# A decoder-trunk step: the last expert pass written out with its own code and an on-chip product, and the state-space input matrices laid out by the host

## The reference

```python
mod = dot(silu(c), ada_w) + ada_b            # 9 condition vectors -> shift, scale, gate, twice
h = LN(x) * (1 + scale1) + shift1
q, k, v, u = split(dot(h, w_in))             # attention beside a state-space layer on u
bbr = cr[..., None] * br - ci[..., None] * bi  # input matrices b_re, b_im: 64 groups x 64 states x 16 channels
x = LN(ALPHA * x + gate1 * o) * ln1_g + ln1_b
h2 = LN(x) * (1 + scale2) + shift2
# hierarchical mixture of 32 experts: each row goes to 2 of them, with weights comb
act = silu(h2 @ w_gate[e]) * (h2 @ w_up[e]) * comb[:, e]
f = sum_e act @ w_down[e]                    # w_gate, w_up: 2048 x 512, w_down: 512 x 2048, each 4 MB
y = LN(ALPHA * x + gate2 * f) * ln2_g + ln2_b
```

## Time and profile before

| | us |
|---|---|
| median of 3 runs | 1608.94 (1608.58 to 1610.85) |
| the profiled execution's own time | 1608.62 |
| its span | 1606.8 |
| TensorE busy in the span | 1493.3 (93%) |
| VectorE, ScalarE, GpSimd busy | 509.9, 288.0, 142.6 |
| DMA | 559.66 MB, 348 GB/s on average |

### The profile page before, as it was taken

How to read it: one execution, slowest core, us unless ns; L and a number is a source line. 1 busy time by engine, 2 the same in 40 slices (tenths; PEclk the granted TensorE clock), 3 DMA queues, 4 the chain that set the end, 5 groups by cost and what they waited for, 6 DMA issues and landing times.

```text
span 1606.8 us, 22161 instructions
## 1 busy us (share of the span) xinstructions
PE 1493.3 (93%) x8151; PEld 645.8 (40%) x8152; DVE 509.9 (32%) x1446; ACT 288.0 (18%) x669; POOL 142.6 (9%) x213
## 2 busy tenths in 40 slices
PE   3999999999999999999999999999999999999974
PEld 2557544455444445333333433333433333333321
DVE  6648344322343347821211212121121211112116
ACT  2221240143123222111211101010010100001011
POOL 6001000321300230000000000000000000000011
PEclk9999999999999898899999999999999999999987
DMA  9995888972487699899999899999979999999955
GB/s 297 381 387 191 308 324 311 317 195 94 168 300 291 220 361 399 363 409 422 421 422 421 333 385 422 422 421 422 422 291 420 421 421 422 422 421 422 422 229 214
DMA packets 119286, 559.66 MB, mean 348 GB/s; under 512 B 15657, under 2 KB 20553, under 8 KB 64921
## 3 DMA queue, kind: packets, MB, share of 16 engines
q1 hardware_dynamic: 100800, 510.20, 79.7%
q0 software_dynamic: 17952, 46.05, 8.5%
q10 hardware_dynamic: 482, 2.70, 0.6%
HBM read 565.78 MB, written 42.37 MB: 378 GB/s over the span
## 4 chain that ended last, share of the span: by engine, by line
PE 79%; DMA 13%; DVE 3%; ACT 2%; issue 1%; POOL 0%; SPq 0%; POOLq 0%; DVEq 0%; ACTq 0%
PE bank L793 24%; PE bank L810 11%; DMA ring<-in_exp_w_up 8%; PE bank L2431 6%; PE bank L755 6%; PE bank L2315 5%; PE bank L2165 4%; PE bank L348 3%; DMA ring<-in_ada_w 3%; PE bank L2358 2%; PE bank L762 2%; DMA ring<-in_w_in 2%; DVE BC L611 1%; PE bank L801 1%; PE bank L2143 1%
## 5 line engine op out<-in xcount | busy, mean ns | idle before, releaser
L793 PE MATMUL bank<-ring,BC 128*64 128x512 f32 x1984 | 470.6, 596 | 5.5 <-DMA ring<-in_exp_w_up 3.2
L793 PEld LDWEIGHTS bank<-ring,BC 128*64 128x64 f32 x1984 | 153.3, 137 | 296.5 <-issue 273.9
L810 PE MATMUL bank<-ring,BC 128*64 128x512 f32 x992 | 219.7, 595 | 16.7 <-ACT BC L716 16.7
L590 DVE COPY MOD<-bank 128x512 f32<-128x512 f32 x32 | 22.1, 692 | 429.0 <-PE bank L762 429.0
L755 PE MATMUL bank<-H,MOD 128*64 128x512 f32 x512 | 131.1, 592 | 0.3 <-DVE H L2025 0.3
L810 PEld LDWEIGHTS bank<-ring,BC 128*64 128x64 f32 x992 | 70.8, 137 | 142.5 <-issue 142.5
L546 POOL DMA_INDIRECT y_dram<-BC,y_row x31 | 30.0, 968 | 946.1 <-DVE y_row L620 861.1
L2431 PE MATMUL bank<-ring,MT 128*128 128x512 f32 x224 | 101.4, 601 | 0.3 <-ACT BC L1381 0.3
L704 ACT COPY MOD<-bank 128x512 f32<-128x512 f32 x32 | 18.8, 587 | 460.3 <-PE bank L762 460.3
L2315 PE MATMUL bank<-ring,MT 128*128 128x512 f32 x192 | 85.4, 598 | 1.0 <-ACT X L1230 1.0
L617 DVE COPY BC<-bank 128x512 f32<-128x512 f32 x31 | 21.5, 692 | 166.1 <-PE bank L810 166.1
(11 more groups left out here) (561 smaller groups left out, 1462.7 us busy)
## 6 DMA issues: line engine op xcount, KB each, us to landing
ring<-in_exp_w_gate SPq DMA_DIRECT2D x128, 1024.0 KB
ring<-in_exp_w_up SPq DMA_DIRECT2D x128, 1024.0 KB
ring<-in_exp_w_down SPq DMA_DIRECT2D x128, 1024.0 KB
ring<-in_ada_w SPq DMA_DIRECT2D x96, 1024.0 KB
ring<-in_w_in SPq DMA_DIRECT2D x20, 1024.0 KB
y_dram<-con POOLq DMA_DIRECT2D x20, 1024.0 KB, 34.2
ring<-in_w_out SPq DMA_DIRECT2D x16, 1024.0 KB
ring<-in_ssm_glu_w SPq DMA_DIRECT2D x4, 1024.0 KB
```

What stands on the lines that cost most here:

```text
L793: mm = pe.matmul(bank[64 * i:64 * i + 64, 2, :], xT[:, q // 2, k % 4, 64 * (q % 2):64 * (q % 2) + 64], ring[:, at, 512 * (k % 4):512 * (k ...
L810: mm = pe.matmul(bank[64 * (c % 2):64 * (c % 2) + 64, 4 + c // 2, :], aT[:, j, :], ring[:, at, 512 * c:512 * c + 512], start=(j == 0), sto ...
```

## The change

1. **Last pass.** The loops run one pass less, and each engine has straight code for the last one. On TensorE this code leaves out the gathering and the transposes of a next pass, and puts in their places the products that spread gate2 (before in the tail), and three transposes of a selection matrix. The result of the last pass is not written to DRAM: it is copied to `YS`, and a matmul with the transposed selection `SWT` (weight where a row's slot is in this pass, else 0) puts it into the output banks, before the gathered results are added to them. The weights in `DW` are 0 for rows that the last pass has (`live`).
2. **Gathers.** ScalarE signals `y_all` when the writes of the passes before the last have landed and the last pass's ninth chunk (the first of down) is used. The gathers go to slots 6 to 9 and 10 of the ring, not 0 to 5.
3. **Start.** The host lays b_re and b_im out as one tensor of 128 rows of 4 KB, loaded by one DMA. The table is cleared by four memsets on VectorE, first in its program, and not on GpSimd. VectorE copies the transposed conditions (`ct_ready`) after the first decay steps.

```diff
@@ expert_loops
-            with eng.Fori(start, start + FULL) as it:
+            with eng.Fori(start, start + FULL - 1) as it:
...
-            with eng.Fori(start + FULL, start + NBLK) as it:
-                with eng.If(extra > it - (start + FULL)):
+            with eng.Fori(start + FULL - 1, start + NBLK - 1) as it:
+                with eng.If(extra > it - (start + FULL - 1)):
@@ moe_dve
-            for b in range(3):
-                for i in range(2):
-                    V.tensor_scalar(DW[:, b, i, :], ident, cwt[:, b, i:i + 1], None, ALU.mult).then_inc(S("dw_ready"), 1)
...
-            expert_loops(dve, body)
+            last = expert_loops(dve, body) + FULL - 1
+            at, live = rsm[:, 0, :, 0:2], rsm[:, 1, :, 0:2]
+            go(V.tensor_scalar(at, slot_f[:, :, :], 2.0 * SLOTS, None, ALU.add),
+               V.scalar_tensor_tensor(out=live, in0=slot_f[:, :, :], scalar=-2.0 * SLOTS, in1=cwt[:, :, :],
+                                      op0=ALU.is_lt, op1=ALU.mult))
+            iota = spread_mid(con[:, C_IOTA:C_IOTA + SLOTS], 2)
+            for b in range(3):
+                w = [t.rearrange("p (h s) -> p h s", h=2) for t in (SW[:, b, :], SW2)]
+                go(*[V.tensor_scalar(w[i], iota, at[:, b, i:i + 1], cwt[:, b, i:i + 1], ALU.is_equal, ALU.mult)
+                     for i in range(2)])
+                V.tensor_tensor(w[0], w[0], w[1], ALU.add).then_inc(S("dw_ready"), 1)
+                dve.wait_ge(S("dw_ready"), b + 1)
+            for b in range(3):
+                for i in range(2):
+                    V.tensor_scalar(DW[:, b, i, :], ident, live[:, b, i:i + 1], None, ALU.mult).then_inc(S("dw_ready"), 1)
+            dve.wait_ge(S("sg_ready"), last + 1)
+            V.tensor_tensor(AC[hi, :], SG[hi, :], bank[hi, 2, :], ALU.mult).then_inc(S("act_ready"), 1)
+            dve.wait_ge(S("y_written"), 16 * last + Y_FILLED)
+            dve.wait_ge(used, last * RING + len(plan) + RING)
+            V.tensor_copy(YS[:, 1, :], bank[:, 5, :]).then_inc(S("dw_ready"), 1)
@@ moe_act
-            act.wait_ge(S("y_written"), 16 * (extra + FULL) + Y_FILLED)
+            last = expert_loops(act, body) + FULL - 1
+            for i in range(5):
+                act.wait_ge(S("g2_ps"), i + 1)
+                dst = G2[:, 512 * i:512 * i + 512] if i < 4 else G2s
+                nc.scalar.copy(dst, bank[:, G2_BANKS[i], :]).then_inc(S("g2_ready"), 1)
+            act.wait_ge(S("g2_ps"), 6)
+            nc.scalar.copy(SWT.rearrange("p b t -> p (b t)"), bank[:, 0, 0:3 * P]).then_inc(S("g2_ready"), 1)
+            act.wait_ge(used, last * RING + len(plan) + 8)
+            nc.scalar.activation(SG[hi, :], bank[0:64, 2, :], ACT.Silu).then_inc(S("sg_ready"), 1)
+            act.wait_ge(S("at_ps"), last + 1)
+            nc.scalar.copy(aT, bank[:, 3, 0:256].rearrange("p (j s) -> p j s", j=4)).then_inc(S("at_ready"), 1)
+            act.wait_ge(S("y_written"), 16 * last + Y_FILLED)
+            act.nop()
+            act.wait_ge(used, last * RING + len(plan) + 9)
             act.nop().then_inc(S("y_all"), 1)
+            act.wait_ge(used, last * RING + len(plan) + RING)
+            nc.scalar.copy(YS[:, 0, :], bank[:, 4, :]).then_inc(S("g2_ready"), 1)
@@ moe_pe: last_weights(k) is called between the products of the last pass, as next_rows(e, k) in the others
+                if k == 4:
+                    pe.wait_ge(S("mod_ready"), 5)
+                    gate2(0)
+                    gate2(1)
+                elif k == 8:
+                    gate2(2)
+                    gate2(3)
+                elif k == 12:
+                    pe.wait_ge(S("g2_ready"), 2)
...
+                    pe.wait_ge(S("dw_ready"), 3)
+                    for b in range(3):
+                        mm = pe.transpose(bank[:, 0, P * b:P * b + P], SW[:, b, :], ident)
+                    mm.then_inc(S("g2_ps"), 1)
...
-            expert_loops(pe, body)
+            last = expert_loops(pe, body) + FULL - 1
+            place = place_of(last)
+            gate_up(last, place, last_weights)
+            down(last, place)
             tail_pe(pe)
 
-        Y = ring[:, 0:6, :].rearrange("p (b i) d -> p b i d", i=2)
+        Y = ring[:, 6:10, :].rearrange("p (b i) d -> p b i d", i=2)
@@ tail_pe
+            pe.wait_ge(S("g2_ready"), 7)
+            pe.wait_ge(S("dw_ready"), 10)
+            def last_rows(b, q, at):
+                h = slice(64 * (q % 2), 64 * (q % 2) + 64)
+                t = slice(32 * q, 32 * q + 32) if b == 2 else slice(0, P)
+                pe.matmul(bank[t, at, :], SWT[h, b, t], YS[h, q // 2, :], start=True, stop=False)
+            for q in range(4):
+                last_rows(2, q, 7)
+            for b in range(2):
+                for q in range(4 - b):
+                    last_rows(b, q, Y_BANKS[b][q])
@@ the start: gpsimd, then vector
-                for i, s in ((0, "ssm_b_re"), (1, "ssm_b_im")):
-                    for h in range(2):
-                        pool.dma_start(Braw[64 * h:64 * h + 64, i, :, :],
-                                       a[s][0].rearrange("(q h) n c -> h n q c", h=2)[h]).then_inc(S("b_in"), 16)
+                pool.dma_start(Braw.rearrange("p c q n -> p (c q n)"), a["ssm_b_rows"]).then_inc(S("b_in"), 16)
...
-                nc.gpsimd.memset(later[:, 0:8192], 0.0).then_inc(S("ab_clear"), 1)
...
-                dve_chain.settle(dve)
-                dve.wait_ge(S("ct_ps"), 1)
-                V.tensor_copy(cT[:, :, 0:NROW], bank[:, 7, 0:KD * NROW].rearrange("p (k r) -> p k r", k=KD))\
-                 .then_inc(S("ct_ready"), 1)
+                for i in range(3):
+                    dve_chain.tick(V.memset(ring[:, PRE_RING + i, :], 0.0))
+                V.memset(ring[:, PRE_RING + 3, :], 0.0).then_inc(S("ab_clear"), 1)
+                dve.wait_ge(S("con_in"), 16)
```

More of the change, by code:

```diff
@@ L772, in turn, with next_rows, gate2, last_weights @@
                 mm.then_inc(S("turn_ps"), 1)
-            def body(e):
-                place = pe.value_load(rint[0:1, bass.ds(e + I_PLACE, 1)], min_val=0, max_val=E - 1)
+            def next_rows(e, k):
+                if k == 4:
+                    pe.wait_ge(S("sel_ready"), e + 2)
+                    gather_rows(0, 0)
+                    gather_rows(0, 1)
+                elif k == 8:
+                    gather_rows(1, 0)
+                    gather_rows(1, 1)
+                elif k == 12:
+                    gather_samples()
+            def gate2(x):
+                r = slice(32 * x, 32 * x + 32)
+                pe.matmul(bank[:, G2_BANKS[x], :], con[r, C_SEL:C_SEL + P], MOD[r, 3, :], start=True, stop=True)\
+                  .then_inc(S("g2_ps"), 1)
+            def last_weights(k):
+                if k == 4:
+                    pe.wait_ge(S("mod_ready"), 5)
+                    gate2(0)
+                    gate2(1)
+                elif k == 8:
+                    gate2(2)
+                    gate2(3)
+                elif k == 12:
+                    pe.wait_ge(S("g2_ready"), 2)
+                    for g in range(4):
+                        r = slice(32 * g, 32 * g + 32)
+                        mm = pe.matmul(bank[r, G2_BANKS[4], :], con[r, C_SEL + P:C_SEL + P + NS], MOD[r, 3, :],
+                                       start=True, stop=True)
+                    mm.then_inc(S("g2_ps"), 1)
+                    pe.wait_ge(S("dw_ready"), 3)
+                    for b in range(3):
+                        mm = pe.transpose(bank[:, 0, P * b:P * b + P], SW[:, b, :], ident)
+                    mm.then_inc(S("g2_ps"), 1)
+            def gate_up(e, place, between):
                 pe.wait_ge(S("xg_ready"), 2 * e + 2)
                 for k in range(KD):
[L778 to L786, removed]
+                    between(k)
                     for i in range(2):
@@ L796, in body, with down @@
                             mm.then_inc(used, 1)
-                turn(e + 1)
+            def down(e, place):
                 pe.wait_ge(S("rint_ready"), since("rint_ready") + 4)
@@ L812, in body, with place_of @@
                     mm.then_inc(used, 1)
+            def place_of(e):
+                return pe.value_load(rint[0:1, bass.ds(e + I_PLACE, 1)], min_val=0, max_val=E - 1)
+            def body(e):
+                place = place_of(e)
+                gate_up(e, place, lambda k: next_rows(e, k))
+                turn(e + 1)
+                down(e, place)
             gather_first(0)
@@ L821, in moe_pe @@
             pe.wait_ge(S("rint_ready"), since("rint_ready") + 4)
[L822 removed]
+            last = expert_loops(pe, body) + FULL - 1
+            place = place_of(last)
+            gate_up(last, place, last_weights)
+            down(last, place)
             tail_pe(pe)
[L825 to L826 removed]
+        Y = ring[:, 6:10, :].rearrange("p (b i) d -> p b i d", i=2)
+        Yq, xq, mq = [ring[:, 10, 512 * i:512 * i + 512] for i in range(2)], X[:, 2, 0:512], st[:, 2, :]
```

(10 more changed lines are left out.)

24 lines of the change are left out of this document (8 added, 16 removed).

## The result

The changed kernel takes 1598.12 us (median of 4 runs, 1596.48 to 1598.97) against 1609.09 (4 runs, 1608.58 to 1610.85): a ratio of 0.9929, 95% interval 0.9916 to 0.9942. That is 11.0 us less; the forecast was 14.4 less.

A forecast was written before the change was run, and what follows sets the result against it. Chain bound 79% by the matrix engine, 13% by DMA; span 1606.8 - 4.5 (start) - 9.9 (tail) = 1592.4, + 1.8 around it + 0.3 to the median = 1594.5 us; range 1589 to 1602.

The forecast's parts named there:

- rival 2: Start: 64-byte runs cost only what the page's rule says, a gain of 1.8 us instead of 4.5; 1597.2 us, chance 0.12.
- (a): Start: b_re and b_im in 4 KB rows instead of 64-byte runs; later chunks land 4.5 us earlier, bounds 0 and 6.
- (b): Start: GpSimd's memset cost VectorE 2.4 to 7.5 us; moving it has the first block ready at 32.3, not 34.7.
- Rival 3: Start: VectorE's memsets (7 us) hold GpSimd up, so its first loads come late; about 1600 us, chance 0.08.
- (c): Ahead of the last pass: leaving the loop takes 4.0 us, the lower clock 2.3; the pass is 2.9 us later.
- Rival 1: Loop exit costs nothing: clock stays up or the pass catches up with weights; 2.9 us earlier, 1591.6 us, chance 0.2.
- Rival 5: Last pass: straight code fetched behind queued weights, TensorE starts it at 1550 instead of 1527; about 1617 us, chance 0.07.
- (d): Tail: gathers issued from 1551.8, not 1559.98; last product ends at 1578.5, not 1588.4, a gain of 9.9 us.

The follow-up runs named there:

- c_rows: Changed kernel with c_re and c_im also laid out by the host, one load in 8 KB rows, no clearing of Cw: 1597.46 us, ratio to before 0.9926.
- tail_alone: Changed kernel with four loads for b_re and b_im and the clearing on GpSimd again; copy of cT stays moved: 1602.03 us, ratio to before 0.9949.
- memset_back: Changed kernel with the table cleared on GpSimd again, the single load for b_re and b_im kept: 1601.15 us (one run).
- late_gathers: Changed kernel with gathers allowed only when the last pass's whole down product is through, not its first chunk: 1604.96 us, ratio to before 0.9975.
- counted_exit: Changed kernel with each engine's second expert loop ending at the count in its register, no pass skipped: 1594.79 us, ratio to before 0.9912.
- warm_exit: Changed kernel with TensorE running one 128 x 256 product in each of the nine skipped passes: 1598.98 us (one run).

## Why the prediction came out as it did

The mechanisms were right, and each was worth less than forecast: 3.2 us at the start for 4.5, and 7.7 at the end for 9.9. The two are told apart at the silu of the pass before the last, which starts at 1510.17 against 1513.40; all behind it is measured against that shift of 3.23. The measured 1598.1 is nearer to rival 2's 1597.2 than to the forecast 1594.5, but not by rival 2's mechanism, which would have left 1.8 us of the start's gain and the whole of the end's.

**(a)** 4.5 us was mis-sized. The step assumed that rows of 4 KB would bring the window to 387 GB/s, and took 300 as its sign; it came to 261, since the loads of the output matrices, named only as a bound, are slow too (c_rows). Over both windows the shortfall went from (387 - 170) x 8 + (387 - 271) x 8 = 2.66 MB to 1.49: 3.0 us at 387 GB/s, as the chunk's landing shows. The sum needed the second window as well, and of both only the part that is these loads'. The estimate by the page "DMA: Bandwidth & Descriptors" of the Trainium skill (section "Why small descriptors are slow (HBM only)") was 1.8 us; the trace lies between the two, and does not agree with either.

**(b)** "The first block is ready at 32.3" came out as 30.0, and the transposes start at 32.51 because of the fourth chunk, which landed later than (a) had it. A right number, then, by luck: two errors cancel. The memset had cost VectorE 3.5 us (from the copy's start to the statistics' end 10.84 us, now 7.35), between my bounds of 2.4 and 7.5. The lower bound was too low because I had priced a statistic at line 919's 0.69 us, and it takes 0.60 (7.20 / 12). The rest is that the copy starts 1.2 us earlier, which the sum had not at all; tail_alone, with only the copy of cT moved, has it at 20.14 instead of 21.03, so 0.9 of the 1.2 come from that order. In memset_back the memset costs 8.2 us where it meets the tensor-scalar operation. That such an operation is held for the whole of a GpSimd instruction is the rule of the Trainium skill in "SBUF — State Buffer", section "Who interferes with whom". The trace agrees on the end of the wait, 0.08 us after the memset's; what happens before the memset's recorded start it leaves open. Rival 3 is out: four memsets of 1.76 us end at 9.95, ahead of everything that waits, and GpSimd's issues keep their 0.5 us.

**(c)** The last pass was forecast 2.9 us later, and is 4.1 (1547.42 + 3.23 - 1546.53). The gap was 4.50 for 4.0, since the load of the pass's place, with the start of the pass, took 1.1 us and not 0.6; the clock's loss was 2.3, as forecast (5.94 - 3.65). The four quarters were priced at 3.43 us each from the earlier trace rows and follow one another at 3.6 here, 0.7 more; gate2's pairs took 1.06 for 0.9, the small products 1.5 for 1.9. The second fall of the clock that was the upper bound, in the wait for silu, came in late_gathers' execution (8.78 us for the down products) and not in the changed kernel's. Rival 1 had been that the gap costs nothing since the pass catches up with its weights; counted_exit shows how much of that is true: without gap and slow quarter 2.9 us of waits for weights appear, so the gap and the clock cost 4.0 us and not 6.8. Rival 5, a fetch of code behind the weights, is not seen: with the gap's cause removed the straight code follows without a stop.

**(d)** First gather 2.27 us after down starts (2.4 forecast), the last pass's product 7.97 after it (7.9), then 4.62 for 4.1: the four narrow products, which I had taken off, take as long as the wide ones (0.598 and 0.609 us each). The samples and both blocks as forecast, but the one more product in block 1 is two instructions of 1.05 us together, not 0.5. With 1.2 from (c) that makes the 2.2 us that are missing from the 9.9. Block 0's rows and TensorE met at 1562.0, as nearly even as forecast. late_gathers bears it out: against the end of the down products its first gather is issued 5.15 us later (0.33 behind it instead of 4.82 ahead), and TensorE waits 4.84 us for block 0.

## What to carry to other kernels

Look at the GB/s beside the DMA share: a full queue that moves half of its usual rate is paid by every load behind it, and the difference to the full rate, summed over the whole stretch and split by who causes it, is the price. Two things that must both be there before an engine can go on don't add, in gain or in loss: price them together, by the later one. When work is moved behind a loop that skips its surplus passes, the way out of the loop stands ahead of it, and costs its own length and the clock after it; end the loop at its count.

## What the runs showed of the hardware

- A skipped pass takes TensorE's sequencer 0.75 us. Of nine of them 3.4 us stood in the open behind the last product (3.44 in the kernel before), the rest under products already queued, and the load of the pass's place behind them made the gap 4.50; with the loop ending at its count (counted_exit) the next product followed at once. A standstill of 4.5 us was followed by the lower clock level, a string of pauses of 0.3 us between small products (warm_exit) was not. The stops of 1.53 and 0.54 us ahead of the last down products were followed by it in late_gathers' execution and in none of the changed kernel, warm_exit and counted_exit.
- VectorE's memset of 128 x 2048 at 6.05 took 1.76 us beside GpSimd's memset of the same size at 5.38 (1.82 us), and neither was longer than by itself (1.76 at 8.19, and 1.82 in memset_back, where VectorE has none); GpSimd's memset of 128 x 8192 beside a VectorE copy or tensor-scalar operation of 32 x 128 made these 7.76 and 8.38 us long instead of 0.21, each to 0.08 us after the memset's end.
- 512 KB in runs of 64 bytes (four loads) cost 3.0 us more than in rows of 4 KB (one load), with the DMA engines full all the time; the other 512 KB, in runs of 256 bytes (sixteen loads), cost about 2.1 us more than in rows of 8 KB, an estimate from the windows.
